# Forget attention in a one-core kernel: the softmax weights normalised inside the turning product instead of on GpSimd

## What is computed

```
s = einsum(q, k) * scale + c[t] - c[s]        # c: running sum of log-sigmoid of the forget logit
p = softmax(s, keys <= t)                     # over the keys
o = einsum(p, v)
```

## Time and profile before

| | us |
|---|---|
| runs of the kernel before | 2696.07, 2696.64, 2703.76 |
| median | 2696.64 |
| profiled execution, its own time | 2694.2 |
| its span | 2692.3 |
| mean granted TensorE clock | 0.929 |

### The profile page before, as it was taken

One profiled execution on the slowest core, in us unless ns is written; L12 is line 12 of the kernel. 1 busy time (PEld: TensorE's weight loads), 2 busy tenths in 40 slices (PEclk: granted clock), 3 DMA queues, 4 the chain that ended last, 5 costly groups with the idle time before them and its releaser, 6 DMA issues.

```text
span 2692.3 us, 40452 instructions
## 1 busy us (share of the span) xinstructions
PE 2473.3 (92%) x16464; PEld 2157.2 (80%) x16464; DVE 1313.0 (49%) x2112; ACT 907.4 (34%) x1395; POOL 869.6 (32%) x756
## 2 busy tenths in 40 slices
PE   7979999978999999999989999999978997889877
PEld 6868888778999999965889999968746786666665
DVE  6465756658726734234487167321244300555423
ACT  4233424233323333356323133322343211444421
POOL 3222323214545540032335455434454420000041
PEclk9879999879999999999989999999999997887788
DMA  3111111011222222210112222322210242000020
GB/s 147 57 47 48 63 48 63 32 42 69 85 96 95 80 102 79 86 41 1 52 61 82 97 94 80 102 78 79 102 40 32 79 125 94 1 0 0 0 94 32
DMA packets 28723, 175.35 MB, mean 65 GB/s; under 512 B 3344, under 2 KB 3856, under 8 KB 11664
## 3 DMA queue, kind: packets, MB, share of 16 engines
q1 hardware_dynamic: 28560, 173.02, 18.3%
HBM read 166.71 MB, written 2.10 MB: 63 GB/s over the span
## 4 chain that ended last, share of the span: by engine, by line
PE 66%; issue 19%; POOL 7%; DVE 4%; ACT 1%; DVEq 1%; POOLq 1%; ACTq 0%; DMA 0%
PE PS L631 17%; PE PS L632 17%; PE PS L633 17%; POOL ring_r L2305 6%; PE PS L1197 3%; PE PD L1011 3%; PE PS L909 2%; PE PS L999 1%; PE PS L1151 1%; POOL arena L2366 1%; DVEq L379 1%; PE PD L939 1%; PE PC L909 1%; PE PS L873 1%; POOLq L2363 1%
## 5 line engine op out<-in xcount | busy, mean ns | idle before, releaser
L2305 POOL TENSOR_TENSOR ring_r<-ring,arena_r 128x512 fp32r<-128x512 f32 (+1 forms) x584 | 776.1, 1360 | 1412.9 <-ACT arena_r L1271 1412.9
L633 PE MATMUL PS<-arena_r,ring_r 128*128 128x264 f32 (+1 forms) x3904 | 1182.1, 303 | 0.0
L633 PEld LDWEIGHTS PS<-arena_r,ring_r 128*128 128x128 f32 x3904 | 751.6, 193 | 23.3
L631 PE MATMUL PS<-arena_r,arena_r 128*128 128x264 f32 (+1 forms) x2464 | 724.5, 294 | 23.0 <-issue 19.9
L632 PE MATMUL PS<-arena_r,arena_r 128*128 128x264 f32 (+1 forms) x2432 | 709.9, 292 | 0.0
L631 PE MATMUL PS<-arena_r 128*128 128x264 f32 (+2 forms) x1792 | 570.9, 319 | 30.4 <-POOL ring_r L2305 13.1
L631 PEld LDWEIGHTS PS<-arena_r,arena_r 128*128 128x128 f32 x2464 | 469.0, 190 | 41.3 <-issue 31.8
L632 PE MATMUL PS<-uT_r,arena_r 128*128 128x264 f32 (+1 forms) x1472 | 474.7, 322 | 0.0
L632 PEld LDWEIGHTS PS<-arena_r,arena_r 128*128 128x128 f32 x2432 | 462.9, 190 | 6.3 <-issue 1.0
L1271 ACT ACTIVATE arena_r<-ring 128x2048 fp32r<-128x2048 f32 (+1 forms) x146 | 261.8, 1794 | 460.7 <-PE PS L633 446.0
L631 PEld LDWEIGHTS PS<-arena_r 128*128 128x128 f32 x1792 | 351.7, 196 | 56.2 <-issue 31.7
(11 more groups left out here) (334 smaller groups left out, 3001.4 us busy)
## 6 DMA issues: line engine op xcount, KB each, us to landing
ring<-stream SPq DMA_DIRECT2D x130, 1024.0 KB, 4.8
ring<-down SPq DMA_DIRECT2D x32, 704.0 KB, 4.1
arena<-arena SPq DMA_DIRECT2D x24, 128.0 KB, 2.9
hT<-x_in SPq DMA_DIRECT2D x4, 528.0 KB, 7.2
arena<-tables SPq DMA_DIRECT2D x4, 512.0 KB, 4.8
out<-uT SPq DMA_DIRECT2D x4, 512.0 KB, 2.8
par<-params SPq DMA_DIRECT2D x1, 1634.5 KB, 13.9
arena<-tables SPq DMA_DIRECT2D x1, 1024.0 KB, 6.3
```

Source lines behind the costliest of these rows:

```text
L631: mm(out_, r32(ah), r32(bh), start=start, stop=False)
L633: return mm(out_, r32(a), r32(bh), start=False, stop=stop)
L2305: last = G.tensor_tensor(r32(low[:, cut]), raw[:, cut], split(high[:, cut]), ALU.subtract)
```

## The change

POOL no longer scales X. It still takes the inverses of the sums, and then writes, for each query tile, a 128x128 diagonal matrix of them (the identity times the column of inverses) into a buffer laid over the idle `uT`. PE's transpose of X against the identity becomes a plain matmul of X against that diagonal, which turns and scales at once. X itself stays unscaled. The semaphores and the order of all engines stay as they were.

```diff
@@ -448,6 +448,8 @@
+        mix_diag = uT[:, :, :].rearrange("p k l -> p (k l)")[:, 0:4 * S].rearrange("p (n e m c) -> p n e m c", n=4, e=2, m=2)
@@ -1049,10 +1051,10 @@
                 for e in range(2):
                     pe.wait_ge(sem("fx_p"), 2 * f + e + 1)
-                    for a, at, w in mix_parts(n):
-                        for b in range(0, w, P):
-                            last = nc.tensor.transpose(PC[:, e, at + b:at + b + P], ev["X"][:, n % 4, e, at + b:at + b + P],
-                                                       ident)
+                    for m, (a, at, w) in enumerate(mix_parts(n)):
+                        for b in range(at, at + w, P):
+                            last = mm(PC[:, e, b:b + P], ev["X"][:, n % 4, e, b:b + P], mix_diag[:, f % 4, e, m, :],
+                                      start=True, stop=True)
                     last.then_inc(sem("fx_t"), 1)
@@ -2361,9 +2363,8 @@
                         r = ev["rs"][:, n % 4, 2 * e:2 * e + len(parts)]
                         G.tensor_tensor(r, r, prm("neg_ones")[:, 0:len(parts)], ALU.pow)
                         pool.drain()
-                        for m, (a, at, w) in enumerate(parts):
-                            x = ev["X"][:, n % 4, e, at:at + w]
-                            last = G.tensor_scalar(x, x, r[:, m:m + 1], None, ALU.mult)
+                        for m in range(len(parts)):
+                            last = G.tensor_scalar(mix_diag[:, f % 4, e, m, :], ident, r[:, m:m + 1], None, ALU.mult)
                         last.then_inc(sem("fx_p"), 1)
```

## The result

The changed kernel takes 2701.57 us in the median of 20 runs (2697.67 to 2706.82), the kernel before 2696.13 us (2694.25 to 2703.76, 20 runs). The ratio is 1.0020 with an interval of 1.0014 to 1.0027: 5.4 us slower, where 1.8 us less was forecast. That is inside the 0.3% that the prediction counted as no change, but clear of the scatter of twenty runs, on the other side, and just above the range. Its profiled execution took 2700.81 us with a span of 2698.8.

What follows compares the result with a forecast made beforehand. PE, busy for 92% of the span, was taken as the bound, with waits deciding in the four edited pairs. Pair changes of -1.28, +0.87, -0.36 and -0.99 us sum to -1.8: 2696.64 becomes 2694.8 us, range 2690 to 2701.

Steps and rivals of the forecast that it cites:

- POOL's part: In the four pairs, 32 scalings become diagonals of 0.64 us; POOL sheds 15.0 us and leaves PE's path.
- PE's part: In the four pairs, 80 transposes become products of 0.252 us each; PE takes on 9.6 us.
- The dear product: Rival: each product's load and multiplication do not overlap, 0.55 us per product, +11.3 us, 2707.9 us; chance 0.08.
- The rule of four: Skill page's claim that float32 transposes are four times faster than products; it would make the sum +8.2 us.
- ACT is what is late next: Before each pair's first group mean, PE's wait for ACT's line 1550 grows from 4.8 to some 8 us.
- The sum, pair by pair: Changes of the four pairs: -1.28, +0.87, -0.36 and -0.99 us, in all -1.8.
- the term: In the third pair, the first group mean cannot start before 2011.22, as ACT's list up to it never waits for POOL.
- the clock falls more often: Rival: three more slow stretches in the pairs, 1.8 us each, +3.6 us, 2700.2 us; chance 0.10.
- The merged wait for ACT: Before the first mean, PE's remaining waits merge into one of 2 us, which might bring a slow stretch.
- The rest costs nothing that I can find: Outside the pairs: no DMA issued or moved, and "eout" and all behind it start earlier by the pairs' gain.
- Part 4: PE-mode transpose: Skill section cited for the rival of a rising clock in the pairs: -4.8 us, 2691.8 us; chance 0.13.

Runs made afterwards that it cites:

- e3: Changed kernel with PE keeping the transposes, diagonals written by POOL, weights' normalisation left out: 2695.94 us, ratio 1.0002 to the kernel before.
- e14: Changed kernel with ACT's copy moved ahead and unread products filling PE's wait for DVE at the pairs' ends: 2695.94 us, ratio 0.9984.
- e9: Changed kernel with two unread 128x512 products in PE's wait for ACT before each pair's first group mean: 2708.53 us, ratio 1.0030.
- e5: Kernel before with one unread 128x512 product, 0.86 us of PE, inside "eout": 2701.59 us, ratio 1.0024.
- e4: Kernel before, POOL still scaling X, with PE's transposes replaced by plain products with the identity: 2705.55 us, ratio 1.0031.
- e11: Changed kernel with ACT's copy of the retention output moved ahead of the pair's last exponentials: 2695.60 us, ratio 0.9989.
- e12: Changed kernel with unread products, 1.3 us, in PE's wait for DVE at the end of each pair but the last: 2695.95 us, ratio 0.9985.
- e15: The same kernel as e11, run again: 2698.15 us, ratio 1.0001 to the kernel before.

## Why the prediction was wrong

**POOL's part** was right: 32 scalings at 0.61 us, 19.3 us (0.64 and 20.5 forecast), all diagonals in time, 0.3 us of waiting left of 12.1.

**PE's part** was right and taken a little too dear: two groups of four in 1.88 us make 0.235 for a product, 0.252 forecast. The dear product is excluded by this. The rule of four from the Trainium skill's "TensorE: Matmul & The Clock Gate", section Terms, does not hold here: 0.235 against 0.13 to the next work is a factor of 1.8.

**"ACT is what is late next"** was right: 8.5 us of waits forecast as some 8.

**The sum, pair by pair, failed in its clock.** It laid the slow stretches of the old profile, with their prices, on the new timeline. At full clock the step from the mean to the last scores took 6.88 us for 7.04, so the account of instructions held. But the stretches moved from where they cost 1.8 us (end of the first pair, head of the second) and next to nothing (last pair, where POOL was late anyway) to places where they cost more: on the products of the second pair, and at the heads of the third and the last. With that the term fell that put the third pair's first mean at 2011.22, as before: it came at 2012.00, in a pair that had begun 1.05 us earlier, and the last pair's came at 2037.12 for 2035.28. The second pair, forecast at +0.87, gained 0.83, and the third, forecast at -0.36, lost 2.66. Together that made +0.8 of -1.8. e3 shows the same for POOL's part: 4.1 us won where the sum gives 7.1. What the change is worth at full clock throughout no run shows; the 86.9 us of e14 have ACT's earlier copy and the fillers in them. My rival "the clock falls more often" came nearest in its number, 2700.2 us at a chance of 0.10, but by luck: it had +3.6 us in the pairs, where 0.8 was measured, and knew nothing of what lies behind. The merged wait for ACT, which it named as the cause, is excluded as the sole one by e9.

**"The rest costs nothing that I can find: 'eout' and all behind it start earlier by what the pairs gave"** is the step that cost most. The step supposed that what lies behind the stage takes the same time whenever it starts. It took 5.8 us more in the first profile and 2.6 in the second, and e5 shows that 0.86 us of delay are enough for it, with none of the change. If the stage's 0.84 us of both profiles hold for the median too, 4.6 of the 5.4 us between the medians are this. No case of the prediction held it, and so the range ended 0.6 us too low.

**The rule in the Trainium skill's "TensorE: Matmul & The Clock Gate", section "Part 4: PE-mode transpose"**, that transposes do not count for the clock as products do, spoke for the change: it would have the full clock more often after it. The clock over the stage fell, 0.95 to 0.93, and in e4, which has only the products more, it stayed at 0.95. Nothing here bears it out.

What stays open: why the chip puts the slow stretches where it does, and so how much a given shift costs. The same kernel had 650.3 and 647.1 us behind the same stage, so one profile tells that part to some 3 us only, and beyond the 2.3 us at the head of the odd layer's projections it is not known what decides. That PE's waits act together in bringing the slow clock is argued from e9, e11, e12 and one profile of e14; both fillings together, without the earlier copy, were not tried, and whether length or number of them counts was not tried.

## What to carry to other kernels

Moving work from an engine that PE waits for onto PE pays only what the next wait leaves: here 12.1 us of waits gave 4.1, as ACT's place in its own list took over and the clock fell a little more, and 80 dearer products took 4.9; look for the queue position that is late next and move it in the same change. In a kernel whose TensorE clock falls and rises, a shift of a microsecond can move the total by five in parts that nobody touched: before believing a change of a few tenths of a per cent, profile both kernels twice, cut the span into the edited stage and the rest, and put a bare delay into the old kernel as a control.

## What the runs showed of the hardware

I had not expected that one 0.86 us product in 2696 us could cost 5.4 us, nor that the stage's length repeats to 0.02 us from run to run, slow stretches included, while the rest of the same kernel varies by 3 us and more (e11 and e15: 89.73 us in both stages, 655.2 and 648.3 behind). Nor that the same sums at the same moment, 2100.1 us, behind the same wait of 4.20 us, run at full or nearly full clock in one kernel (1.19 us) and at half in another (2.08 us), whose edit lies over 50 us earlier. Nor that short waits of PE, none over 2.4 us in this stage of the kernel before, go with stretches at 1.2 GHz (0.91 to 0.96 over the stage of the changed kernel with the wait of 1.3 us at the pairs' ends or the wait for ACT left as it was), while the one version with the first filled and the second shortened ran its four pairs at 2.4 GHz throughout (1.00); that the waits are the reason is likely, not shown.
